# Two weight homes held back before the experts, eleven projections by seven products, and the eighth expert home in one stretch

## The reference, cut to what matters

```python
# first block ("b1"): gated linear attention beside block attention, then a conv FFN
h = rmsnorm(x, norm_mix)
qa, ka, va, ra, a_lr, qb, kb, vb, gates = split(h @ w_in)   # 512, 512, 1024, 1024, 16, 512, 512, 512, 2048
log_a = log_sigmoid(a_lr @ w_lr_up + b_forget) / 16
oa = gla_chunked(qa, ka, va, log_a)                          # chunks of 64 tokens, 4 heads
oa = rmsnorm_per_head(oa) * silu(ra)
ob = moba_attention(qb, kb, vb, rel_bias)                    # 8 heads of 64
x = x + (sig(g_a) * (oa @ w_a) + sig(g_b) * (ob @ w_b)) @ w_out
x = x + ffn_with_conv(rmsnorm(x))
# second block ("b2"): stick-breaking attention and pooling, memory attention, experts
q, k, v, u = split(rmsnorm_2(x) @ w_in_2)                    # 512 each
x = x + concat(stick_breaking(q, k, v), pool(u)) @ w_out_2
x = x + memory_cross_attention(...)
x = x + moe_ffn(...)                                         # 32 experts, top 4, three 1024x1024 matrices each
# third block: two layers ("l0", "l1"), each SwiGLU, attention, memory attention, SwiGLU
```

## Time and profile before

| | |
|---|---|
| median of 3 runs | 3085.13 us (3085.05 to 3087.13) |
| time of the profiled execution | 3085.77 us |
| its span, first to last instruction | 3084.0 us |
| PE busy | 2938.8 us, 95% |
| DVE busy, ACT busy | 1233.8 us (40%), 591.2 us (19%) |
| mean granted PE clock | 0.987 of full speed |
| loads of experts | 192 chunks of 2 MB, mean rate over the whole span 234 GB/s |

### The profile page before, as it was taken

One profiled execution on the slowest core, in us unless ns is written; L12 is line 12 of the kernel. 1 busy time (PEld: TensorE's weight loads), 2 busy tenths in 40 slices (PEclk: granted clock), 3 DMA queues, 4 the chain that ended last, 5 costly groups with the idle time before them and its releaser, 6 DMA issues.

```text
span 3084.0 us, 42888 instructions
## 1 busy us (share of the span) xinstructions
PE 2938.8 (95%) x17806; PEld 2232.3 (72%) x17806; DVE 1233.8 (40%) x2405; ACT 591.2 (19%) x1195; POOL 13.0 (0%) x22
## 2 busy tenths in 40 slices
PE   8999999999999889899888999999999999999999
PEld 5888889768543343343344599986899999977999
DVE  2131456322311111111111466655566665643565
ACT  2110321131211111111111210143210110242210
POOL 0000000000000000000000000000000000000000
PEclk9999999999999999999999999999999999999999
DMA  7333435323799999999999744541344444532341
GB/s 298 134 113 137 184 144 192 136 88 128 307 426 426 426 426 426 426 426 426 426 426 424 306 169 176 205 150 55 118 177 171 164 168 173 210 120 110 137 165 69
DMA packets 63209, 723.71 MB, mean 235 GB/s; under 512 B 6908, under 2 KB 7036, under 8 KB 22480
## 3 DMA queue, kind: packets, MB, share of 16 engines
q1 hardware_dynamic: 59472, 705.74, 57.6%
q0 software_dynamic: 3584, 15.74, 1.5%
HBM read 720.32 MB, written 1.12 MB: 234 GB/s over the span
## 4 chain that ended last, share of the span: by engine, by line
PE 84%; DMA 11%; ACT 2%; DVE 1%; issue 1%; SPq 0%; POOL 0%; DVEq 0%; ACTq 0%
PE ps L558 65%; PE ps L1410 8%; DMA sb_weights<-stream 6%; PE ps L1434 5%; DMA sb_o<-stream 3%; DMA sb_a<-stream 2%; PE ps L1388 2%; PE ps L1350 2%; PE ps L848 1%; DVE sb_x L2343 0%; PE ps L1378 0%; ACT sb_k L1954 0%; DVE sb_h L2099 0%; ACT sb_tr L1599 0%; ACT sb_o L1599 0%
## 5 line engine op out<-in xcount | busy, mean ns | idle before, releaser
L558 PE MATMUL ps<-sb_h,sb_weights 128*128 128x256 f32 (+1 forms) x3856 | 712.7, 342 | 20.2 <-DMA sb_weights<-stream 8.6
L558 PEld LDWEIGHTS ps<-sb_h,sb_weights 128*128 128x128 f32 x3856 | 625.6, 192 | 90.9 <-DVE sb_h L2099 12.8
L1410 PE MATMUL ps<-sb_weights,sb_k 128*64 128x512 f32 x1280 | 339.9, 595 | 21.9 <-ACT sb_k L1954 13.1
L2690 DVE TENSOR_TENSOR sb_v<-ps,sb_small 128x256 f32<-128x256 f32 x128 | 48.5, 420 | 677.1 <-PE ps L1378 677.0
L1410 PEld LDWEIGHTS ps<-sb_weights,sb_k 128*64 128x64 f32 x1280 | 110.1, 137 | 214.8 <-issue 214.8
L1410 PE MATMUL ps<-sb_a,sb_k 128*64 128x512 f32 x512 | 226.6, 596 | 6.8 <-DMA sb_o<-stream 5.4
L1434 PE MATMUL ps<-sb_weights,sb_k 128*64 128x512 f32 x640 | 181.4, 626 | 38.4 <-DMA sb_weights<-stream 24.2
L558 PE MATMUL ps<-sb_o,sb_weights 128*128 128x256 f32 x768 | 172.0, 385 | 8.4 <-ACT sb_o L1599 6.9
L558 PE MATMUL ps<-sb_a,sb_weights 128*128 128x128 f32 (+1 forms) x1232 | 171.0, 297 | 1.1 <-DVE sb_a L2509 1.1
L558 PEld LDWEIGHTS ps<-sb_o,sb_weights 128*128 128x128 f32 x768 | 147.1, 193 | 31.8 <-ACT sb_o L1599 7.3
L558 PEld LDWEIGHTS ps<-sb_a,sb_weights 128*128 128x128 f32 x1232 | 160.1, 192 | 8.2 <-issue 1.5
(11 more groups left out here) (389 smaller groups left out, 3794.1 us busy)
## 6 DMA issues: line engine op xcount, KB each, us to landing
sb_weights<-stream SPq DMA_DIRECT2D x262, 2048.0 KB, 8.9
sb_a<-stream SPq DMA_DIRECT2D x48, 2048.0 KB, 26.3
sb_ex<-stream SPq DMA_DIRECT2D x24, 512.0 KB, 22.6
sb_tr<-stream SPq DMA_DIRECT2D x24, 512.0 KB, 23.6
sb_v<-stream SPq DMA_DIRECT2D x24, 512.0 KB, 24.4
sb_o<-stream SPq DMA_DIRECT2D x24, 512.0 KB, 26.2
sb_a<-tables POOLq DMA_DIRECT2D x2, 2048.0 KB, 16.7
sb_a<-tables POOLq DMA_DIRECT2D x2, 1536.0 KB, 14.1
```

What stands on the lines that cost most here:

```text
L558: ins = pe.matmul(out, lhsT, rhs, start=start, stop=stop, skip_group_check=skip)
L1410: ins = pe.matmul(ps[own[e], :], XG[:, k * PAIR + e * LOT:k * PAIR + (e + 1) * LOT], w[e](k * 512, 512), start=k == 0, stop=k == KT - 1)
L2690: ins = dve.tensor_tensor(by_lot(z, s), by_lot(PS[TURNED[c][0]][:, :], s), bias.unsqueeze(3).broadcast_to([P, 2, 2, LOT]), ALU.add)
```

## The change

Three things at once.

1. Before the experts only `W[0]` to `W[2]` take weight chunks (`PRE_SLOTS = 3`). `W[3]` and `W[4]` serve as scratch: the spare buffers for the combinations, the token sums and the kept parts. Their first expert chunks are loaded when k2 has been scaled and v2 is out; in SP's queue this stands behind the last early chunk.
2. Eight chunks of the first block (ka, va twice, qb, kb, vb, ra twice) and three of the second (u2, k2, v2, in this new order) go through `project_seven`. What stood between the halves of a plain chunk stands between whole ones, but for `forget_gates`, which PE does ahead of the last product of ka. `first_sums` moves ahead of u2. The copies by `scale_units` and `copies_v` go.
3. `EX`, `TR`, `V` and `O` become parts of one tile `SHARED`, so that the eighth expert home is one stretch of 4096 columns and takes one transfer of 2 MB.

```diff
-        moe_slots = [[w[:, :]] for w in W] + [[A[:, 0:CH]], [A[:, CH:2 * CH]],
-                                              [EX[:, :], TR[:, :], V[:, 2048:3072], O[:, 1024:2048]]]
+                                              [SHARED[:, 2048:2048 + CH]]]
...
-        moe_order = [(MOE_FIRST + j) % SLOTS for j in range(SLOTS)] + list(range(SLOTS, MOE_SLOTS))
+        late_order = [3, 4] + [(MOE_FIRST + j) % PRE_SLOTS for j in range(PRE_SLOTS)]
+        moe_order = late_order + list(range(SLOTS, MOE_SLOTS))
...
+        spare = [W[PRE_SLOTS][:, i * 1024:(i + 1) * 1024] for i in range(4)]
+        SUMS_AT = {"b1": W[PRE_SLOTS + 1][:, 0:2048], "b2": W[PRE_SLOTS + 1][:, 0:2048], "l0": A[:, 6144:8192], "l1": R[:, 0:2048]}
...  PE, first block
-            fm("ka", h, 1, between={0: forget_gates})
-            tm("va", h, 2, between={0: bias_tables, 1: forget_sums})
+            project_seven("b1", 0, forget_gates)
+            project_seven("b1", 1)
+            forget_sums()
+            bias_tables()
+            project_seven("b1", 2)
             keys_and_scores()
-            fm("qb", h, 1, between={0: state_sums})
-            fm("kb", h, 1, between={0: gla_values})
-            tm("vb", h, 1)
+            project_seven("b1", 3)
+            state_sums()
+            project_seven("b1", 4)
+            gla_values()
+            project_seven("b1", 5)
             for g in range(4):
                 banks.wait_emptied(pe, ("gla_o", g))
-            fm("ra", h, 2, between={1: lambda: sums("n_gla")})
+            project_seven("b1", 6)
+            sums("n_gla")
+            project_seven("b1", 7)
...  PE, second block
-            fm("k2", h, 1, between={1: lambda: first_sums("n_mix2")})
-            tm("v2", h, 1)
-            fm("u2", h, 1)
+            first_sums("n_mix2")
+            for i in range(3):
+                project_seven("b2", i)
...  ACT
+            project_kept("b1", 7, first_gates)          # first_gates: roots("n_gla"), then Silu of ra, units 0 and 1
...  DVE, first block
+            def first_projected(l, name):
+                norm_done(dve, name)
+                sum_tokens([SUMS_AT[l][:, j * 512:(j + 1) * 512] for j in range(4)])
+                project_combine(l, 0)
+            late_norm("n_mix", ..., lambda: first_projected("b1", "n_mix"))
             scale_units("qa", Q, range(2))
...
-            scale_units("ka", K, [0])
+            project_combine("b1", 1)
             for t in range(2):
                 ...                                     # LOGA, waits for gla_softplus t + 1
-            scale_units("ka", K, [1])
+            project_out("b1", 0)
+            project_combine("b1", 2)
+            project_out("b1", 1)
...
             norm_out("n_gla")
-            scale_units("ra", R, range(2, 4))
+            project_out("b1", 7)
...  DVE, second block
-            late_norm("n_mix2", seven_added("w_down"))
+            late_norm("n_mix2", seven_added("w_down"), lambda: first_projected("b2", "n_mix2"))
             scale_units("q2", Q, range(2), 0.125)
+            project_combine("b2", 1)
+            project_out("b2", 0)
+            project_combine("b2", 2)
             first_norm("n_mix2")
-            scale_units("k2", R[:, 4 * T:], range(2))
-            scale_units("u2", R, range(2))
+            project_out("b2", 1)
...                                                      # pooling, in the same place
+            project_out("b2", 2)
...  SP
-            for c in range(1, SLOTS):
+            for c in range(1, PRE_SLOTS):
...
-                if n < SLOTS:
+                if n == 0:
+                    units_scaled(sp, "k2", 2)
+                    banks.wait_emptied(sp, ("v2", "common", 0))
+                elif SLOTS - PRE_SLOTS <= n < SLOTS:
                     sp.wait_ge(released, MOE_FIRST + n - SLOTS + 1)
```

More of the change, by code:

```diff
@@ L34 @@
 SLOTS = 5
+PRE_SLOTS = 3
 NEG = -1e30
@@ new lines, in build @@
+        four = [O[:, 0:1024], O[:, 1024:2048], V[:, 2048:3072], EX[:, :]]
+        spare = [W[PRE_SLOTS][:, i * 1024:(i + 1) * 1024] for i in range(4)]
+        FOUR_SPARE = {"b1": spare, "b2": spare, "l0": four, "l1": four}
+        SUMS_AT = {"b1": W[PRE_SLOTS + 1][:, 0:2048], "b2": W[PRE_SLOTS + 1][:, 0:2048], "l0": A[:, 6144:8192], "l1": R[:, 0:2048]}
+        kept_early = [W[PRE_SLOTS + 1][:, 2048 + i * T:2048 + (i + 1) * T] for i in range(4)]
+        kept_late = [TR[:, i * T:(i + 1) * T] for i in range(4)]
@@ L536, in build, with project_buffers @@
+        def project_buffers(l, i):
+            return [FOUR_SPARE[l][(3 * i + j) % 4] for j in range(3)]
         BY_SEVEN = FT // 2
@@ L909, in seven_products, with project_seven @@
                 end_chunk()
-            def project_seven(l, i):
-                part, c = PROJECTED[i]
-                name, by_token = f"{l}_{part}", part == "v"
+            def project_seven(l, i, between=lambda: None):
+                name, c = PROJECTED[l][i]
+                by_token = name in BY_TOKEN
                 g = sevens[0]
@@ L1186, in state_sums @@
                     banks.wait_emptied(pe, ("kend", t))
-                for u in range(4):
-                    banks.wait_emptied(pe, ("va", u))
+                for c in range(2):
+                    banks.wait_emptied(pe, ("va", "common", c))
                 for c in range(3):
@@ L1341, in _ @@
             first_lots.base[:] = banks.fills[0:4]
-            first_lots.loaded_base[:] = [sum(1 for c in range(MOE_FIRST) if c % SLOTS == s) for s in range(SLOTS)] + [0] * (MOE_SLOTS - SLOTS)
+            first_lots.loaded_base[:] = loads_early
             for t in range(2):
@@ L1902, in _ @@
             token_factors("n_mix2")
-            copies_v("v2", 1, 512, 2048, late=True)
+            for i in range(3):
+                project_kept("b2", i)
             act.add_instruction(mybir.InstLoadActFuncSet(act_func_set_id=6, name=nc.get_next_instruction_name(),
@@ L2294, in project_out @@
                 banks.wait_emptied(dve, (name, "common", c))
-                if part != "v":
+                if not by_token:
                     factor = FACTOR.unsqueeze(1).broadcast_to([P, 2, T])
@@ L2493, in _ @@
                     banks.wait_emptied(dve, ("kv", c, u))
-            scale_units("qb", Q[:, 4 * T:], [1], 0.125)
-            scale_units("kb", K[:, 4 * T:], range(2))
-            scale_units("ra", R, range(2))
+            for i in range(4, 7):
+                project_combine("b1", i + 1)
+                project_out("b1", i)
             norm_out("n_gla")
-            scale_units("ra", R, range(2, 4))
+            project_out("b1", 7)
             dve.wait_ge(sem("ra_act"), 4)
```

186 lines of the change are left out of this document (108 added, 78 removed).

## The result

The kernel after takes 3090.47 us (median of 20 runs), the one before 3085.56 (20 runs): ratio 1.0016, 95% interval 1.0010 to 1.0023. It is 4.9 us slower; the forecast was 2.6 us faster. The profiled execution took 3091.18 us (span 3089.4) against 3085.77 (3084.0), 5.4 us more, near the medians' 4.9. In the rows of after, L585 is before's L558, L1421 is L1388 (gathering the tokens of a pair), L1443 and L1467 are L1410 and L1434; `sb_shared` holds V, EX, TR and O.

What follows compares the result with a forecast made beforehand. PE was taken to bound the kernel before the experts, the weight stream in them. Terms -0.5 + 2.5 + 0.4 + 1.0 - 6 = -2.6 us took the median from 3085.13 to 3082.5 us; range 3075.5 to 3091.

Steps and rivals of the forecast that it cites:

- The last pair is bound by PE, so nothing is counted there.: Last pair of experts: the faster weight stream's gain was counted as nothing there.
- a load that comes late: Slower rival, at the w_down combination: DVE does not catch up, 8 us; 3090.5 to 3094, chance 0.08.
- Stall behind ka: First block, before va: PE idle 8.7 us, because DVE takes LOGA, which waits for ACT, ahead of ka's additions.
- sevens pay: Faster rival, first block: DVE's additions behind ka don't wait for ACT and the clock holds; 3072.2, chance 0.07.
- Clock behind it: Behind the stall before va: granted clock falls to 0.50, 2.5 us lost, ends 0 and 6.8.
- First block without the clock: First block up to the second pair's logits: 0.5 us gained after stall and waits, clock loss not counted.
- the second wait: At the attention, before the second pair's logits: PE wants the bank at 171.7 and starts at 173.5.
- the price of a chunk: Both blocks: plain chunk 13.9 us, by seven products 12.51 (by feature) or 12.1 (by token); 16.8 us less without waits.
- Second block: u2, k2, v2 up to the first head: 0.4 us slower through waits, plus 1.0 for the clock (0 to 1.7).
- Experts: Expert weight stream: eighth home in one transfer saves 0.29 us in each of 21 refills, 6 us (0 to 9.6).
- The rival: Same time, experts: by the skill's line-rate rule the pieces lose nothing, so no gain; 3088.5, chance 0.12.
- Three homes: Ahead of the experts: three weight homes cost 0, DVE's slack covering one late load; without cover up to 8 us.

Runs made afterwards that it cites:

- experiments 1 to 3: Code-place runs: never-entered branch lengthened in the kernel after (experiment 1) and before (experiment 2); third: after repeated 3090.82 us, and with 16 instructions added 3085.47 us.
- experiment 6: Kernel before with three weight homes instead of five ahead of the experts, plain chunks, eighth home in four pieces: 3085.74 us, ratio 1.0003.
- experiment 4: Kernel after with DVE's additions of ka's chunk taken ahead of the two LOGA operations: 3082.97 us, ratio 0.9983 of before.
- experiment 5: Kernel before with only the eighth expert home in one stretch, loaded by one transfer, run twice: 3080.3 us (ratio 0.998) and 3077.73 us (0.9972).
- experiment 8: Kernel after with ka's additions first, code moved, roots of n_gla earlier, second block plain; run twice: 3074.71 us (0.9963 of before) and 3074.51 us (0.9960).
- experiment 2: Kernel before with 104 instructions added inside the branch that is never entered: 3089.22 us, ratio 1.0008.
- experiment 1: Kernel after with 64 instructions added inside the branch that is never entered: 3086.74 us, ratio 0.9995 of before.
- the dose of 16: Kernel after with 16 instructions added inside the branch that is never entered: 3085.47 us, ratio 0.9996 of before.

## Why the prediction was wrong

The step that failed is in the experts: "The last pair is bound by PE, so nothing is counted there." The seven products made PE's program longer, and the branch's target came to lie near the end of a fetched piece of code. That was no term of the sum and none of the rivals: the pair was put at nothing without asking what the 7.24 us are in which PE stands idle there already before the change. It costs 3.7 to 5.35 us (experiments 1 to 3), enough to turn the sign of -2.6. The other 2 to 4 us of the miss are, by the traces, in the first block's term and in half-clock stretches, below.

That 3090.47 still lies inside the stated 3075.5 to 3091 is luck: the upper end stood there for a load that comes late, and experiment 6 measures that at nothing. Three of the signs were missed: the second logits at 177.41 (173.5 to 177), the first head at 597.01 (592 to 596), and 428 GB/s in the experts for 430.

Point by point, forecast and trace:

- **Stall behind ka**: 8.7, measured 8.24 on PE; taking it away brought 7.5 us (experiment 4). Right, place and cause too. The forecast's "sevens pay" rival needed just this stall away and had 3072.2; with the stall away and the code moved the kernel takes 3076.93.
- **Clock behind it**: 2.5, measured 2.0 (3.95 us of work at half clock).
- **First block without the clock**: -0.5 forecast. The second logits moved by 3.39, less 0.37 of start and 2.0 of clock: +1.0. The term was mis-sized by 1.5 us, although the second wait was met (1.75 for 1.8). Most of it is the price of a chunk: from its first product to what follows, a chunk by feature takes 12.50 to 12.97 us (`qb` 12.70, from 85.36 to 98.06) for 12.51, and the eight, without waits and without what the clock took, come to 100.0 us by the rows where the sum had 98.8. `state_sums` took 4.84 us from 98.06 on, 0.9 more than before, where 0.4 was taken.
- **Second block**: +0.4 and 1.0 for the clock. Waits of 0.9, 2.7, 1.2 forecast, 0.94, 2.53, 1.17 measured; +1.0 in all. The clock term came to nothing between the traces, because before's has such a stretch in q2 (20 matmuls took 6.27 us, in after's 4.58); that the sum of the two is near is luck.
- **Experts**: -6 forecast, 5.1 us less between the marks in after and 5.6 in experiment 5, where the kernel gained 6.2 and 8.6. Right. The rival took up the Trainium skill, "DMA: Bandwidth & Descriptors", Specifications, which gives 512 B as the smallest transfer that runs at line rate. That pieces of 4 KB a partition lose nothing, as the prediction read it, did not hold here: both intervals of experiment 5 lie below 1. That the pieces' size and not their number of transfers did it was not told apart.
- **Three homes**: 0 forecast, 1.0003 measured; the late load came as described, and DVE's slack covered it.

The edits' own runs make up the result: homes 0, one stretch -6.2 to -8.6, the code's place +3.7 to +5.35, and so by difference some +6 to +10 for the seven products in the order of the change, of which 7.5 were the additions behind LOGA. In the two traces the clock falls differently at four places: +1.6 ahead of the experts, +1.6 in the last pair, +1.7 at 2053.0, -5.05 at 2131.1.

## What to carry to other kernels

Seven products in place of eight pay only where nothing waits for the additions: list for each chunk what stands ahead of the additions on DVE, and put them before anything that waits for a third engine. Where DVE has no pause between two blocks' work, a reordering only moves the stall to the next chunk, so leave that block plain. After any edit that lengthens an engine's program, look behind each jump for a gap that waits for nothing, and shift the code by some instructions if one is there. Where a stretch at half clock comes in some executions and not in others, compare executions of the same mean granted clock, or the time between two marks on both sides of the edit's place.

## What the runs showed that was not expected

- A branch over code that is not entered has a price that hangs on the place of its target. In all fourteen traces PE stands 7.2 to 7.7 us at it, and the branch alone takes 5.9 to 6.4 of them; the first matmul starts within 0.2 us behind it in each, so the picked tokens are not what PE stands for. Where five or six instructions are left of the piece by the program lengths, it stands another 4.5 to 5.3 us (4.47, 4.98, 5.07 and 5.29 us in four traces), against none in the other ten, before and those with 16 or more added among them. One packet of instructions moves during the branch too; that its 6 us are the fetch of a piece was not tested.
- The expert loop itself fetches next to no code: three packets of instructions in 780 us.
- The length of the half-clock stretch ahead of the experts differed between executions of one and the same kernel: 17.1 and 13.7 us in after and its repetition, 20.5 and 13.7 in experiment 8's two. It is worth up to 3.4 us, as much as some of the edits, so one trace against one trace can't settle those.
- A stretch of 10.2 or 13.7 us at half clock near 2120 to 2148 is in five of the fourteen traces (before, experiments 1, 4 and 8 twice). Kernels that execute the same instructions differ in it: before has it and experiment 2 not, experiment 1 has it and the dose of 16 not. What decides it was not found.
